# Sums of squares for the cross-attention queries: GpSimd adds in place of column-group matmuls on TensorE

## The reference, cut to what matters

```
def rms_norm(x, g):
    xf = x.astype(jnp.float32)
    y = xf * lax.rsqrt(jnp.mean(xf * xf, axis=-1, keepdims=True) + EPS)
    return (y * g.astype(jnp.float32)).astype(x.dtype)

def cross_sublayer(x, mem_k, mem_v, lp):
    hn = rms_norm(x, lp["norm_x_pre"])
    q = jnp.einsum("bsd,dhe->bshe", hn, lp["w_xq"])
    s = jnp.einsum("bshe,bmhe->bhsm", q, mem_k).astype(jnp.float32) * MEM_SCALE
    ...
    x = x + rms_norm(y, lp["norm_mix_post"])     # end of the mixer, just ahead
```

## Time and profile before

| | us |
|---|---|
| median of 3 runs | 1190.46 (1188.66 to 1192.6) |
| profiled execution | 1187.28 |
| its span in the trace | 1185.6 |
| PE busy | 1133.7 (96%) |
| DVE busy | 894.6 (75%) |
| ACT busy | 643.4 (54%) |
| POOL busy | 172.8 (15%) |

### The profile page before, as it was taken

The page is one execution under the profiler, slowest core; times in us unless marked ns, Lnnn a source line. Parts: engine busy times, 40 slices in busy tenths (PEclk is TensorE's granted clock), DMA queues, the critical chain, the costliest instruction groups (busy, mean ns, idle before and its releaser), DMA issues. The chain is left out here.

```text
span 1185.6 us, 25819 instructions
## 1 busy us (share of the span) xinstructions
PE 1133.7 (96%) x10203; PEld 1058.5 (89%) x10203; DVE 894.6 (75%) x1530; ACT 643.4 (54%) x1130; POOL 172.8 (15%) x282
## 2 busy tenths in 40 slices
PE   6999999999999999999879999999999999999988
PEld 6999999999777899997869999999997779999877
DVE  5789998899867544687587999889998674448856
ACT  7474454645557444565665644454545664446554
POOL 1210101010353000032011010101014520001310
PEclk9999999999999999999989999999999999999999
DMA  7795746475668466687347767564754765667852
GB/s 211 189 268 139 223 131 182 132 190 137 168 190 243 141 184 182 184 259 271 116 113 197 212 162 203 151 179 129 193 153 143 231 202 148 184 189 213 279 195 74
DMA packets 318971, 216.13 MB, mean 182 GB/s; under 512 B 21620, under 2 KB 300512, under 8 KB 318298
## 3 DMA queue, kind: packets, MB, share of 16 engines
q1 hardware_dynamic: 301728, 164.64, 50.4%
q0 software_dynamic: 16800, 49.83, 13.3%
q10 hardware_dynamic: 330, 0.11, 0.0%
HBM read 209.31 MB, written 7.15 MB: 183 GB/s over the span
## 5 line engine op out<-in xcount | busy, mean ns | idle before, releaser
L1327 ACT ACTIVATE whi<-stage 128x2048 fp32r<-128x2048 f32 (+2 forms) x157 | 272.9, 1739 | 272.6 <-PE U L691 228.7
L1950 DVE TENSOR_TENSOR wlo<-stage,whi 128x2048 fp32r<-128x2048 f32 x138 | 315.8, 2289 | 129.2 <-ACT whi L1327 129.1
L689 PE MATMUL U<-Ahi,whi 128*128 128x264 f32 x1152 | 331.7, 288 | 1.2 <-DVE wlo L1950 0.5
L690 PE MATMUL U<-Alo,whi 128*128 128x264 f32 x1152 | 326.6, 284 | 0.0
L691 PE MATMUL U<-Ahi,wlo 128*128 128x264 f32 x1152 | 326.1, 283 | 0.0
L689 PEld LDWEIGHTS U<-Ahi,whi 128*128 128x128 f32 x1152 | 217.1, 188 | 3.7 <-DVE wlo L1950 1.6
L690 PEld LDWEIGHTS U<-Alo,whi 128*128 128x128 f32 x1152 | 217.2, 189 | 0.0
L691 PEld LDWEIGHTS U<-Ahi,wlo 128*128 128x128 f32 x1152 | 216.2, 188 | 0.0
L2127 DVE SCALAR_TENSOR_TENSOR acc<-uext,cwall,acc 128x256 f32<-128x256 f32 x464 | 189.3, 479 | 0.4
L689 PE MATMUL U<-Bhi,whi 128*128 128x264 f32 x384 | 108.9, 284 | 0.0
L690 PE MATMUL U<-Blo,whi 128*128 128x264 f32 x384 | 108.8, 283 | 0.0
(11 more groups left out here) (462 smaller groups left out, 2171.3 us busy)
## 6 DMA issues: line engine op xcount, KB each, us to landing
stage<-in_w_in SPq DMA_DIRECT2D x76, 1024.0 KB, 6.0
stage<-in_w_out SPq DMA_DIRECT2D x32, 1024.0 KB, 5.9
stage<-in_w_mk SPq DMA_DIRECT2D x8, 1024.0 KB, 6.2
cp<-in_cache_kv_latent POOLq DMA_DIRECT2D x64, 128.0 KB, 3.2
cp<-in_cache_kv_latent SPq DMA_DIRECT2D x64, 128.0 KB, 2.9
stage<-in_w_mv SPq DMA_DIRECT2D x8, 1024.0 KB, 5.4
Kt<-in_cache_mem_k POOLq DMA_DIRECT2D x16, 512.0 KB, 5.9
stage<-in_w_xq SPq DMA_DIRECT2D x8, 1024.0 KB, 7.0
```

The lines of the kernel that those rows point to most:

```text
L689: mm(bk[:, 0:cols], whi[:, s, w], hi[:, k, :], start=(k == 0), stop=False)
L690: mm(bk[:, 0:cols], whi[:, s, w], lo[:, k, :], start=False, stop=False)
L1327: return A_(out, in_, ACT.Copy, scale=scale)
L1950: ins = V.tensor_tensor(wlo[:, s, :], stage[:, s, :], whi[:, s, :].bitcast(F32), ALU.subtract)
```

## The change

GpSimd makes the sum over the chunks. `add_up(q)`, placed in POOL's list behind `store_rows` 0, 2, 4 and 5 and ahead of the `load_keys` there, waits for `sq_rdy` of quarter q and adds its squares to a tile `sqPair` of two chunks: one addition of 128x528 for the first quarter, two for each other one, each waiting for the one before it. After the last, one addition of 128x264 folds the two chunks into `sqs`: eight instructions in a layer. PE's four groups of column-group matmuls and ACT's copy `partial(l, 5)` go; PE's matmul of ones by `sqs` stays at its place and waits for the eighth addition. The root's scale changes, since `ST` had held each sum 32 times.

```
+    sqPair = at("sqPair", [P, 2, T], M)
...
+    sum_add = C("sum_add", 8)
...
+            def add_up(q):
+
+                sq = yg[:, 4 * q:4 * q + 4, :]
+                wait_apart(pool, sq_rdy.sem, sq_rdy.at(l, 5 + q))
+                if q == 0:
+                    nc.gpsimd.tensor_tensor(sqPair[:, :, :], sq[:, 0:2, :], sq[:, 2:4, :], ALU.add).then_inc(sum_add.sem, 1)
+                else:
+                    for e in range(2):
+                        wait_apart(pool, sum_add.sem, sum_add.at(l, 2 * q + e - 1))
+                        nc.gpsimd.tensor_tensor(sqPair[:, :, :], sqPair[:, :, :], sq[:, 2 * e:2 * e + 2, :], ALU.add
+                                                ).then_inc(sum_add.sem, 1)
+                if q == 3:
+                    wait_apart(pool, sum_add.sem, sum_add.at(l, 7))
+                    nc.gpsimd.tensor_tensor(sqs[:, :], sqPair[:, 0, :], sqPair[:, 1, :], ALU.add).then_inc(sum_add.sem, 1)
+
             wait_apart(pool, stat.sem, stat.at(l, 6))
             for s in range(2 * MH - 1):
                 store_rows(s)
+                if s in (0, 2, 4, 5):
+                    add_up((0, 2, 4, 5).index(s))
                 if s in (0, 2, 4, 5):
                     load_keys((0, 2, 4, 5).index(s))
...
             for q in range(4):
                 pe.wait_ge(h_lo.sem, h_lo.at(l, 9 + q))
                 part(U_XQ, 0, Bhi[:, :, :], Blo[:, :, :], 4 * q, 4 * q + 4)
-                pe.wait_ge(sq_rdy.sem, sq_rdy.at(l, 5 + q))
-                last = group([yg[:, 4 * q + c, :] for c in range(4)], q == 0, q == 3)
                 if q == 0:
                     mem_rows(7)
-            last.then_inc(part_mm.sem, 1)
...
             part(U_XQ + 1, 1, *XB, 0, 4)
-            combine(7, 5)
+            pe.wait_ge(sum_add.sem, sum_add.at(l, 8))
+            mm(ST[:, 0:T], ones[:, :], sqs[:, :], start=True, stop=True).then_inc(stat.sem, 1)
             part(U_XQ + 1, 1, *XB, 4, KC)
...
             for h in range(MH):
                 step(U_XQ + h, h)
-                if h == 0:
-                    partial(l, 5)
                 if h < 3:
                     hi(U_XQ + h + 2, h)
                 if h == 0:
-                    root(stat.at(l, 7), l, rsq.at(l, 5), 1.0 / (32 * D))
+                    root(stat.at(l, 7), l, rsq.at(l, 5), 1.0 / D)
```

More of the change, by code:

```diff
@@ L280, in build @@
     h_lo = C("h_lo", 12, 0, natural=True)
-    part_mm = C("part_mm", 5, -1, natural=True)
-    part_ev = C("part_ev", 5, -1, natural=True)
+    part_mm = C("part_mm", 4, -1, natural=True)
+    part_ev = C("part_ev", 4, -1, natural=True)
+    sum_add = C("sum_add", 8)
     sv_rdy = C("sv_rdy", 2)
@@ L1374, in partial @@
             act.wait_ge(part_mm.sem, part_mm.at(l, r))
-            act.wait_ge(stat.sem, stat.at(l, (0, 2, 3, 4, 6)[r - 1]))
+            act.wait_ge(stat.sem, stat.at(l, (0, 2, 3, 4)[r - 1]))
             copy(sqs[:, :], ST[:, 0:T]).then_inc(part_ev.sem, 1)
```

## The result

The changed kernel is slower. In six executions each, its median is 1204.23 us against 1188.94 for the kernel before: 15.3 us more, a ratio of 1.0121 with a 95% interval of 1.0106 to 1.0136. The range of the prediction, 1187.3 to 1208.0, holds it. The forecast of 1200.5 is 3.7 us short; as a difference to the kernel before, 10.0 us were forecast and 15.3 measured.

A forecast was written before the change was run, and what follows sets the result against it. PE was taken to set the pace, busy 29.6 of 30 us, with DVE nearly full. Holding's +10.0 on the profiled 1187.28 gave 1197.3; with 3.2 for the median, 1200.5 us, range 1187.3 to 1208.

The forecast's parts named there:

- The holding of DVE: Query stretch: DVE loses each GpSimd addition's length, second query unit 5.0 us a layer later, 10.0 in all; chance 0.54.
- a = 1.1: Length in us of one GpSimd addition of 128x528, taken as what DVE loses when it falls in busy time.
- the formula: Second query unit's delay a layer: 7a - 2.7 us, from seven additions before the end of `wlo`.
- bounds of 0.63 and 1.62: Limits in us for one GpSimd addition: half a DVE addition of 128x1056, and three times a memset of 128x512.
- What was hidden: GpSimd's own list: additions finish at 521.9, PE asks for `sqs` at 523.4, so 1.5 us of cover.
- The code load: Ahead of GpSimd's first addition: 1.28 us by ACT's table load, costing nothing; about 6 us by the skill's price.
- The removal: PE's four column groups a layer, 0.68 us each with the first worth nothing, and ACT's 0.39 us copy go.
- The 1.36 us a layer at the second unit: PE's gain without holding: second query unit starts at 521.85 in place of 523.21, limited by `wlo`.
- 1.15 us a layer, 2.3 in all, with nothing set against it: Removal's worth in time, taken between PE's gain of 1.36 and 0.84 on the fourth query unit's weights branch.
- one term, 10.0: Holding's cost over both layers at the second query unit, 5.0 us each, with the groups' removal inside this sum.
- the clock: PE waits of 5 us in the query stretch could lower PE's granted clock; price put inside the range's upper end.

The follow-up runs named there:

- removal_alone: The changed kernel without the GpSimd additions and TensorE's wait for them, the sum of squares left out: 1188.99 us, ratio 0.9996 to the kernel before.
- removal_padded: removal_alone with 16 one-column fp32 matmuls at the kernel's start and 16 at the second layer's start: 1191.32 us, ratio 1.0018 to the kernel before.
- removal_late: removal_alone with 32 small fp32 matmuls at the second layer's start and none at the kernel's start: 1185.43 us, ratio 0.9975 to the kernel before.
- adds_alone: The kernel before plus the eight GpSimd additions a layer, column groups and copy kept, TensorE not waiting for the additions: 1197.31 us, ratio 1.0076.
- changed_filled: The changed kernel with 16 full-width fp32 matmuls of constants a layer where TensorE waits: 1198.47 us, ratio 1.0077 to the kernel before.
- changed_late: The changed kernel with 32 small fp32 matmuls at the second layer's start: 1198.3 us, ratio 1.0079 to the kernel before.
- half_width: The changed kernel with all additions of one chunk, 128x264, half of the squares left out: 1192.1 us, ratio 1.0028 to the kernel before.
- write_only: The changed kernel with each GpSimd addition replaced by a memset of about its length, sum left out: 1191.62 us, ratio 1.0026 to the kernel before.
- one_operand: The changed kernel with each GpSimd addition replaced by a one-operand copy, the sum left out: 1191.07 us in one execution.
- changed_padded: The changed kernel with 16 one-column fp32 matmuls at the kernel's start and 16 at the second layer's start: 1206.57 us, ratio 1.0135 to the kernel before.

## Why the prediction was right, and where it was short

*The holding of DVE.* Right, and nearly to the number. The prediction took a = 1.1 for what an addition takes from DVE; it is 1.0 to 1.06, with 0.57 for the fold, which the formula had left out. With these the formula gives 7 x 1.03 + 0.57 - 2.7 = 5.1 us a layer at the second unit, 5.0 was forecast, and 5.02 and 5.09 were measured. That a came out so near is in part luck: it was the middle of bounds of 0.63 and 1.62, taken from a DVE addition and a memset, and it was meant as the addition's own length. The additions are listed with 1.29 us and more, and hold DVE for less than that. What proves the mechanism is not the agreement but the set: memsets of the same place and length leave DVE alone, half the width takes half, and without any waiter the cost stays. The rule of the Trainium skill (SBUF — State Buffer, "Who interferes with whom") is that a VectorE instruction with two SBUF inputs contends with a GpSimd instruction that reads SBUF, and not with one that only writes it; the trace agrees in all of these. The same section calls the shared ports an exclusive lock; for VectorE's two-port modes it writes: "Whoever issues first gets the shared pair for the whole instruction". The prediction took that over to two inputs. Here the trace agrees less well: the additions of 506.12 and 513.27 let a second DVE instruction pass, and the copy held DVE for half of its shortest listed length.

*What was hidden.* The additions on GpSimd's own list were: TensorE has no wait at the matmul of `sqs`. The code load ahead of the first addition cost nothing that the trace shows: GpSimd was idle for 2.24 us before it in the first layer and for 2.16 in the second, where there is no such load. The 6 us that the Trainium skill gives (GPSIMD Engine Reference, section 2.1) did not come here.

*The removal.* The 1.36 us a layer at the second unit were measured as 1.39 and 0.98 in removal_alone, 1.37 and 1.36 in removal_padded, and 0.48 and 1.33 in removal_late; why the two smaller ones are smaller was not found. The step "1.15 us a layer, 2.3 in all, with nothing set against it" failed as a time: taken alone the removal gave nothing. With the list's length restored it gives 3.4, with an interval of 1.8 to 4.0, which holds the 2.3. So it is the removal's second effect, the shifted instruction list, that the prediction lacked.

*The missing 5 us.* The forecast summed one term, 10.0. The runs put 8.8 to 9.5 on it (adds_alone 8.8, changed_filled and changed_late 9.5). So the 1204.23 lies in the range for another reason than the one given: the range reached to 1207.8 because an addition might have cost DVE 1.62 us, and it cost 1.03. The other 6 us lie in TensorE's clock and in the longer gap. The prediction named the clock and put it inside the upper end without a price; it did not name the fetch at all. The Trainium skill has the fetch (Runtime: NRT & Kernel Launch, "Instruction fetch mechanics"): the list is refilled in blocks of 256 instructions, at a cost that is mostly hidden. 64 matmuls with their 64 weight loads are half such a block, so by its rule the removal puts the block's border elsewhere; that agrees with a gap that keeps its place in the list, and with packets of 16,384 bytes at the gaps. That the cost is hidden agrees with 0.42 us in the second layer of the kernel before, less well with 0.99 in its first, and not with 2.69 in the changed one, where the whole way from the fetch's start to TensorE's next matmul (2.45 us) lies open.

The parts can be read off the two profiles, which lie 18.1 us apart: 2.3 for the clock in the first layer, 0.35 for it in the second, 2.3 for the longer gap, about 1 for the clock behind that, and 1.5 for the clock at 904 us; the rest is the holding. That clock and fetch together make the 6 us agrees with changed_filled and changed_late, which have neither of these costs in their profiles. How much each makes of it in the median is not shown: in one profile against another the clock's first-layer part differs by 2.3 us with the same instructions.

## What to carry to other kernels

GpSimd is no free engine beside a VectorE that works on two SBUF operands: count what it reads as time taken from VectorE, and put its reading work where VectorE is idle or where its slack exceeds it. An edit that takes instructions out of a full TensorE list moved the places where TensorE stood still for its instruction fetch, and one of these gaps grew by 2.3 us; before a result of 2 us is believed, try the same kernel with the list's length restored by dead instructions in a wait. When an engine begins to wait in the middle of a dense stretch, look for the clock behind the wait and for whether anything hides it.

## What the runs showed of the hardware

- A GpSimd addition of 128x528 fp32 is listed with 1.29 us at the shortest, always beside a running VectorE instruction, and held a two-operand one for 1.0 to 1.06; one of 128x264 0.75 us, and 0.57 (0.44 for `xT` in half_width). A copy of 128x528 is listed with 0.63 us at the shortest and held for 0.31. A memset of 128x1024 took 0.95 us and held nothing.
- In the second layer's matmuls of `ST<-KTB,qm` TensorE stands still once without waiting for an engine or for data. The gap is 2.43 to 3.18 us in the five kernels that have 64 matmul records less by then (changed, removal_alone, write_only, half_width, one_operand), always behind 117 of these matmuls, and 0.34 to 1.22 us in the nine that have the old count, behind 172 or 173. It comes where the list is used up fastest, 64 matmuls in about a microsecond. It is an instruction fetch: TensorE goes on 2.3 to 2.6 us behind the start of a 16,384-byte packet of the instruction queue, and the long gaps are those whose packet starts late. What sets its start was not tried.
- 16 one-column fp32 matmuls with a full block of weights, listed as 32, took 6.99 us at the kernel's start (removal_padded, 0.44 each) and 3.63 us at the start of the second layer (changed_padded, 0.23 each). The granted clock is listed with 1.00 for both; no run shows what makes the first ones slower.
